# Three order changes in a one-core decoder step: ScalarE rounds weight pieces ahead of the pooling evictions, VectorE's two middle heads become a hardware loop, and two loads move down SyncE's queue

## The reference, cut to what matters

```python
h = rmsnorm(x, g_mix)
z = h @ w_in                       # columns: u 512 | q 512 | k 512 | v 1024 | gate_a 1024 | gate_b 1024
pool_out, new_hist = pool_mixer(u, ...)            # windowed means of u, times w_pool
ret, s_new = retention(rotary(q), rotary(k), v, state)   # 4 heads, chunks of 128 rows, a state per head
mixed = sigmoid(ga) * pool_out + sigmoid(gb) * head_group_norm(ret)
x = x + mixed @ w_out
h2 = rmsnorm(x, g_ffn)
x = x + hier_moe(h2, ...)          # router, 32 experts, top 2 of one group
y = rmsnorm(x, g_final)
```

## Time and profile before

| | |
|---|---|
| median of 3 runs | 1025.19 us (1023.0 to 1025.54) |
| profiled execution, its own time | 1025.19 us |
| its span in the profile | 1023.5 us |
| TensorE busy | 962.8 us (94%) |
| VectorE busy | 740.1 us (72%) |
| ScalarE busy | 443.4 us (43%) |
| GpSimd busy | 218.5 us (21%) |

### The profile page before, as it was taken

The page is one execution under the profiler, slowest core; times in us unless marked ns, Lnnn a source line. Parts: engine busy times, 40 slices in busy tenths (PEclk is TensorE's granted clock), DMA queues, the critical chain, the costliest instruction groups (busy, mean ns, idle before and its releaser), DMA issues.

```text
span 1023.5 us, 16141 instructions
## 1 busy us (share of the span) xinstructions
PE 962.8 (94%) x5326; PEld 833.0 (81%) x5327; DVE 740.1 (72%) x1626; ACT 443.4 (43%) x738; POOL 218.5 (21%) x223
## 2 busy tenths in 40 slices
PE   4999999999999999999998999969999999999970
PEld 4898888988889888898886888847888888888860
DVE  4874557845578455784558755589999999999965
ACT  6611113011130111311114122138988988998864
POOL 0001220012200122001221100031434443443320
PEclk9999999999999999999999999979999999999995
DMA  8611105111051110501118342389999999999938
GB/s 280 214 31 53 42 22 184 32 53 42 22 182 32 53 41 24 181 32 57 58 60 272 133 165 84 110 308 409 397 389 394 396 397 387 394 397 385 342 52 331
DMA packets 74723, 190.21 MB, mean 186 GB/s; under 512 B 12503, under 2 KB 47555, under 8 KB 62227
## 3 DMA queue, kind: packets, MB, share of 16 engines
q1 hardware_dynamic: 61403, 159.66, 41.3%
q0 software_dynamic: 13248, 29.62, 9.9%
HBM read 167.43 MB, written 38.68 MB: 201 GB/s over the span
## 4 chain that ended last, share of the span: by engine, by line
PE 88%; DMA 5%; DVE 3%; ACT 1%; issue 1%; SPq 1%; POOL 0%; DVEq 0%; POOLq 0%; ACTq 0%
PE bank L1975 17%; PE bank L867 13%; PE bank L869 12%; PE bank L868 12%; PE bank L1976 9%; PE bank L898 8%; PE bank L1038 3%; PE bank L1964 1%; PE bank L938 1%; PE bank L1990 1%; PE bank L1998 1%; PE bank L1986 1%; PE bank L1994 1%; DMA xall<-in_x_prompt_dram 1%; DMA x<-sum_d 1%
## 5 line engine op out<-in xcount | busy, mean ns | idle before, releaser
L1328 DVE TENSOR_TENSOR w_lo<-w,w_hi 128x1024 fp32r<-128x1024 f32 x128 | 150.3, 1215 | 0.1
L756 ACT ACTIVATE w_hi<-w 128x1024 fp32r<-128x1024 f32 x128 | 129.8, 1068 | 3.0 <-PE bank L869 2.9
L1975 PE MATMUL bank<-wvg_hi,hT_hi 128*128 128x512 f32 x256 | 104.4, 408 | 0.0
L867 PE MATMUL bank<-w_hi,xT_hi 128*128 128x512 f32 x256 | 102.9, 402 | 1.3 <-issue 1.3
L1975 PE MATMUL bank<-wvg_lo,hT_hi 128*128 128x512 f32 x256 | 100.9, 394 | 0.0
L1975 PE MATMUL bank<-wvg_hi,hT_lo 128*128 128x512 f32 x256 | 100.7, 393 | 0.0
L869 PE MATMUL bank<-w_hi,xT_lo 128*128 128x512 f32 x256 | 100.3, 392 | 0.0
L868 PE MATMUL bank<-w_lo,xT_hi 128*128 128x512 f32 x256 | 99.7, 390 | 0.0
L1794 ACT ACTIVATE v<-bank 128x256 f32<-128x256 f32 x32 | 12.3, 383 | 201.3 <-PE bank L1976 201.3
L2319 POOL TENSOR_TENSOR mixed<-onorm,pgate 128x256 f32<-128x256 f32 x36 | 39.6, 1100 | 271.6 <-DVE onorm L2137 271.6
L867 PE MATMUL bank<-hT_hi,wuqk_hi 128*128 128x344 f32 x288 | 94.4, 328 | 0.2 <-DVE hT_lo L2057 0.2
(11 more groups left out here) (273 smaller groups left out, 2379.2 us busy)
## 6 DMA issues: line engine op xcount, KB each, us to landing
w<-in_w_dram SPq DMA_DIRECT2D x96, 1024.0 KB
raw<-in_w_in_dram SPq DMA_DIRECT2D x60, 256.0 KB, 3.2
xall<-in_x_prompt_dram SPq DMA_DIRECT2D x8, 512.0 KB, 8.2
mixed_d<-mixed POOLq DMA_DIRECT2D x32, 128.0 KB, 3.4
sample_state<-in_state_ret_dram SPq DMA_DIRECT2D x16, 256.0 KB, 3.7
out_dram<-sample_state SPq DMA_DIRECT2D x16, 256.0 KB, 3.4
mixed_in<-mixed_d SPq DMA_DIRECT2D x8, 512.0 KB, 4.4
x_again<-in_x_prompt_dram SPq DMA_DIRECT2D x8, 512.0 KB, 3.5
```

Of the source, the lines that this page charges most:

```text
L756: act.activation(hi, whole_w, ACT.Copy).then_inc(S["up_hi"], 1)
L867: pe.matmul(out, lhs[0], rhs[0], start=first, stop=False)
L1328: dve.tensor_tensor(lo, whole_w, hi, ALU.subtract).then_inc(S["up_lo"], 1)
L1975: g = pe.matmul(gates, x[xi], wvg[wi][:, 1:3, k, :], start=first, stop=last)
```

## The change

On ScalarE each of the three u evictions of heads 1 to 3 gets three pieces ahead of it: 6 to 8 before n = 0, 9 to 11 before n = 1 (these stood behind it), 12 to 14 before n = 2 (these stood behind it). On VectorE heads 1 and 2 become the body of a hardware loop, so that counts in their waits and addresses that depend on the head are computed in registers. On SyncE mixed tile 2 and x tile 1 are loaded behind the router loads.

```diff
@@ first_loads_c
             elif i == 1:
                 load_x(sp, 0)
                 load_mixed(sp, 1)
-            elif i == 2:
+            elif i == 3:
+                router_loads(sp)
                 load_mixed(sp, 2)
                 load_x(sp, 1)
-            elif i == 3:
-                router_loads(sp)
@@ ScalarE, head
                     else:
-                        if n != 1:
-                            for q in range(6, 9) if n == 0 else range(9, 12):
-                                round_piece(act, q, h, None)
+                        for q in range(6 + 3 * n, 9 + 3 * n):
+                            round_piece(act, q, h, None)
                         act.wait_ge(S["uqk_mm"], after(9 * h + n + 1))
...
-                for q in range(16 if first else 12, 18):
+                for q in range(16 if first else 15, 18):
                     round_piece(act, q, h, None)
@@ VectorE
             head(0, True, False)
-            for h in range(1, H - 1):
+            with dve.Fori(1, H - 1) as h:
                 head(h, False, False)
             head(H - 1, False, True)
```

## The result

The change makes the kernel slower: 1036.32 us median (1034.43 to 1037.86, 4 runs) against 1024.55 (1023.0 to 1025.54, 4 runs). The ratio is 1.0108, interval 1.0086 to 1.0132, so +11.1 us (8.8 to 13.5). The forecast was 1030.3, range 1026.2 to 1034.5: right in sign, less than half the size, and the time lies above the range. The profiled execution took 1037.92 us with a span of 1036.2, 12.7 more than before. It is one of the longest of the 21 executions of this kernel on record (1030.70 to 1038.70 us, median 1035.93), so its stretches show what the change can cost and somewhat more than it costs as a rule.

What follows compares the result with a forecast made beforehand. The prediction took TensorE, full through the heads, as the bound. It summed 0.76 + 1.0 + 0.4 + 2.8 + 0.15 = 5.1 us onto 1025.2 us, giving 1030.3 us, range 1026.2 to 1034.5.

Steps and rivals of the forecast that it cites:

- Part 1: ScalarE's order, heads 1 to 3: TensorE waits for the later second u eviction; 0.76 us in all.
- Register work at the ends of heads: VectorE's register counts at the ends of heads 1 and 2 delay the starts of heads 2 and 3: 1.0 us.
- Score masks: Register counts ahead of VectorE's score masks in heads 1 and 2 delay TensorE: 0.4 us (0 to 2.6).
- The jump back: VectorE's loop, head 1 to head 2: an instruction load makes the low parts of pieces 6 to 8 2.8 us late.
- by part 1, for TensorE: Head 2: the 2.8 us delay reaches TensorE through the second u eviction, needed for product n = 3.
- SyncE's queue: Turn into stage C: the gain on the sample states is given back by mixed tile 2 landing later; +0.15 us.
- The second rival: Turn into stage C: last router load stands as before, TensorE waits for mixed tile 2; +2.5 us, 1032.7 us; 17%.
- the first rival: VectorE's loop: the jump from head 1 to head 2 costs nothing; 2.3 us in all, 1027.5 us; 20%.
- the fourth: Turn into stage C is won: mixed tile 2 lands by 554.7, TensorE gains 1.6 us; 1028.5 us; 8%.

Runs made afterwards that it cites:

- Alone, part 1: Kernel before with only ScalarE's new rounding order: 1025.66 us, ratio 1.0015.
- the run with a fixed address: Kernel after, with the head's eight columns copied from head 1's fixed address in both loop turns: 1034.07 us, ratio 1.0096.
- the hint: Kernel after, with a hint on VectorE's loop that its back edge will be taken: 1032.53 us, ratio 1.0079.
- part 2 alone: Kernel before with only VectorE's loop over heads 1 and 2, ScalarE in its old order: 1027.75 us, ratio 1.0035.
- part 3 alone: Kernel before with only mixed tile 2 and x tile 1 loaded behind the router loads: 1027.2 us, ratio 1.0034.
- The filled run: Kernel after, with matmuls on constants ahead of product n = 3 in head 2 and ahead of mixed tile 2: 1033.45 us, ratio 1.0085.
- parts 1 and 2: Kernel before with ScalarE's new order and VectorE's loop, SyncE's queue as before: 1031.29 us, ratio 1.0066.
- the fastest version: Kernel before, with mixed tile 2 and x tile 1 loaded behind the state loads but ahead of the router loads: 1023.25 us, ratio 0.9986.
- The run with both repairs: Kernel after, with the back-edge hint and mixed tile 2 and x tile 1 between state and router loads: 1026.83 us, ratio 1.0040.

## Why the prediction was wrong, step by step

**Part 1 (0.76 us): mechanism right, size low.** The second eviction does stand where the third stood, and TensorE waits for it in each head: 0.42 us in head 1 and 0.49 in head 3 (forecast 0.39 and 0.19). Each wait costs 0.16 to 0.17 more than it lasts: product n = 3 is 0.59 and 0.65 us late. That is one step of the stream, whose matmuls take 0.32 us and come 0.16 apart, so the first one behind a wait has nothing to overlap with. Alone, part 1 costs 1.5 us (0.1 to 3.0), which by itself doesn't exclude 0.76; its loads, and so this wait, differ from head to head (0.21 to 1.13 us late).

**Register work at the ends of heads (1.0 us): placed wrong.** From the last state update but one to `sample_queries` VectorE takes 13.17 us before (272.64 to 285.81) and 13.18 after (274.71 to 287.89). The 35 counts in the waits cost nothing there. The work shows in one place, the copy of the head's columns, with an address and two counts from registers: 0.35 us ahead of it and 0.40 behind, where before the three steps follow each other 0.04 and 0.03 us apart (315.91 to 315.95, 316.12 to 316.15). The score masks read at register addresses too, behind other work, and in head 1 no new gap over 0.04 us stands ahead of them. It passes to the kT rotation and to TensorE, which waits 0.4 and 0.5 us in heads 1 and 2; the run with a fixed address has no such wait.

**Score masks (0.4 us): near.** From `project(0)` to the second score product it is 13.26 us in heads 1 and 2 after, 13.13 before: 0.13 each.

**The jump back (2.8 us): right.** 2.51 us of stand (2.28 to 2.51 in the five traces of the loop without the hint), 2.62 of wait on TensorE. Two instruction packets move from 287 to 294 us, none there in the kernel before, and with the hint both the packets and the stand are gone; so it is a load of instructions. The Trainium skill ("Runtime: NRT & Kernel Launch", section "Instruction fetch mechanics") says that a taken branch to a block that isn't held forces a load; the trace now agrees, with 2.51 us, or 2.28 with part 2 alone. But "by part 1, for TensorE" was too narrow: without part 1 TensorE is caught at the sample states, 1.93 us, and head 2 loses 4.38 us all the same.

**SyncE's queue (0.15 us): the step that failed.** It was "with 1 MB less ahead this should end earlier by what the state load saves". In the kernel after the last router load held the queue 3.16 us instead of 3.82: 0.66 us earlier, not 1.9. With part 3 alone it was free sooner, after 1.99 us, but then mixed tile 2 was itself held for 1.55, 3.54 in all. So the wait for room didn't go with the 1 MB; the prediction let tile 2 go out at once. The second rival had it nearer, that the router loads fill the queue and not the 1 MB: the stand is there without the 1 MB, and it passes to mixed tile 2 itself when that is next. Its price, +2.5 us, was high for the wait alone (+1.59 from tile 1 to tile 2), and low with what follows it.

**What the sum lacked: the clock.** This is the larger failure. Every term entered the sum as the length of a stand or a delay, and what TensorE does behind it was put at nothing, without a reason. Behind the two long ones TensorE ran 3.4 us at half clock, 1.64 us each, 3.3 in all. The filled run shows it: same start of product n = 3, full clock, both stretches 1.6 us shorter. The trace of before gave no warning where I looked: its stand of 1.54 us at the sample states left the clock at 1.00. It did further on: in the router's stage, where TensorE waits 1.14 and then 4.08 us, the clock is at 0.50 for some 10 us (windows).

```profile
673.40:683.50 10.10, 4.82 (x34) 4.00 (x35) 8.40 (x37) 7.10 (x11) 1.81 (x3) 0.50 0.82 341
```

**The two sums.** Forecast 5.1. Measured in the traces: 1.65 (head 1) + 5.33 (head 2) + 1.61 (head 3 and its end) + 1.59 + 1.64 = 11.8, with 0.42 ahead of the heads and 0.50 in the experts. The step that most raised it over the forecast is the half clock (3.3), then the queue (1.4), then the copy of the columns, which with the rest between product n = 3 and `project(0)` costs 0.82 us in head 1 and 0.70 in head 2 (in place of 1.0 at the heads' ends). Mixed tile 1 adds 0.69, which no term of the forecast had. (The low end of the range doesn't follow from its own words: the first rival with half of the fourth is 1027.5 - 0.9 = 1026.6, not 1026.2.)

**What stays open.** At mixed tile 1 TensorE waits with no releaser named: 0.3 us before, 0.96 after, 2.1 with parts 1 and 2, 0.63 in the fastest version. The traces name it all the same: in each of these the tile's own load landed 0.09 to 0.10 us before TensorE went on, and it was 6.8, 7.6, 8.6 and 7.2 us on its way. What makes this load longer no run told. At both ends of the span the trace of after has a stretch at half clock that the trace of before lacks, near 20 and near 702 us; the second goes with the 0.50 us in the experts. It stands as well in the traces with part 2 alone, part 3 alone, parts 1 and 2, and the hint, but not in the other traces with parts of the change, so it is tied to no part. The 0.42 us ahead of the heads was not traced further. And when the clock falls is not settled, see below.

## What to carry to other kernels

Price a stand of an otherwise full TensorE at its length plus a restart, and look for a second charge: in this kernel 1.6 us lost to half clock in a full stream, behind most stands of two us or more. Rolling a long body into a loop cost a load of instructions at the jump back, some 2.5 us here, and if the engine has no slack there another engine finds it, wherever the work queues up next. Before a load is moved down a queue, see which issues on it are held and put the urgent load ahead of the first one that is held, as the fastest version here does.

## What the runs showed of the hardware that was not expected

- Behind a stand TensorE's clock was at 0.50 for 3.4 us, after waits of 1.93, 2.07 (mixed tile 1, parts 1 and 2), 2.62, 2.77, 3.24, 3.84 and 3.94 us (the last at mixed tile 2 with the fixed address, where it began 0.6 us ahead of the wait's end); in the run with the hint, at the wait of 3.67 us for mixed tile 2, for 6.8 us, a part of it during the wait. It stayed at 1.00 after waits of 2.11 and 2.86 us, in other runs. So the length of the wait does not decide by itself.
- With the hint on the back edge VectorE doesn't stand at the jump (2.51 us without it) and queue 14 brings no instructions in the loop's second turn, but VectorE stands 1.91 us in the head behind the loop. The run with both repairs shows the same (last packet at 226.39, 1.91 us at 445.00).
- A short VectorE instruction with an address and two wait counts from registers, behind other short ones, had 0.75 us of idle time around it (0.35 + 0.40 against 0.04 + 0.03); with the address fixed 0.25 (0.22 + 0.03) was left. In head 2 with the hint the gap behind it was 0.13, not 0.40. Some 35 counts from registers at the end of a head cost nothing that the trace shows (13.18 against 13.17 us).
- A 512 KB load that was next behind three of the router loads was held at its issue for 3.30 us; with room the issue takes 0.4.
